# Two-block transformer kernel: values of the last attention stationary and split in two, probabilities scaled by GpSimd, a new order of its units, x kept in DRAM

## What is computed

```python
s_c = einsum("bqgid,bngd->bqgin", qc, k_cmp) * scale      # 31 compressed keys
p_c = masked_softmax(s_c, m_c)
o_c = einsum("bqgin,bngd->bqgid", p_c, v_cmp)
...
p_s = masked_softmax(s_s, m_s)        # selected branch: with 512 tokens all 8 blocks are selected
o_s = einsum("bqginl,bqgnld->bqgid", p_s, vg)
...
p_w = masked_softmax(s_w, m_w)        # window of 512: all earlier tokens
o_w = einsum("bqgik,bkgd->bqgid", p_w, vw)
return g[..., 0:1] * o_c + g[..., 1:2] * o_s + g[..., 2:3] * o_w
```

## Time and profile before

| | |
|---|---|
| median of 3 runs | 2189.94 us |
| profiled execution, its own time | 2193.54 us |
| its span | 2191.7 us |
| PE busy | 2092.1 us (95%) |
| DVE busy | 1007.5 us (46%) |
| ACT busy | 748.0 us (34%) |
| POOL busy | 0.2 us (0%) |
| queries of p = 0, first matmul to last rotation | 1768.7 to 1817.7 us |
| rounds, up to the first step of the last product | 1817.7 to 2138.5 us |
| last product and final norm | 2138.5 to 2191.7 us |

### The profile page before, as it was taken

The page is one execution under the profiler, slowest core; times in us unless marked ns, Lnnn a source line. Parts: engine busy times, 40 slices in busy tenths (PEclk is TensorE's granted clock), DMA queues, the critical chain, the costliest instruction groups (busy, mean ns, idle before and its releaser), DMA issues.

```text
span 2191.7 us, 23331 instructions
## 1 busy us (share of the span) xinstructions
PE 2092.1 (95%) x9943; PEld 1703.2 (78%) x9943; DVE 1007.5 (46%) x1342; ACT 748.0 (34%) x1143; POOL 0.2 (0%) x4
## 2 busy tenths in 40 slices
PE   7999999999999999999999999999999988988888
PEld 6899975778787887788888788888887765666666
DVE  4443444424343346542344555555545535555443
ACT  4554551332323233331242222222222123345542
POOL 0000000000000000000000000000000000000000
PEclk9999997999999999999999999999999998999999
DMA  5212122122222222333333333333333350000100
GB/s 192 78 58 77 59 76 67 61 98 77 82 96 75 89 95 87 97 96 96 96 96 96 96 96 96 96 96 96 96 96 112 99 136 20 20 20 20 39 11 39
DMA packets 177384, 177.15 MB, mean 81 GB/s; under 512 B 4609, under 2 KB 154369, under 8 KB 177281
## 3 DMA queue, kind: packets, MB, share of 16 engines
q1 hardware_dynamic: 175088, 170.31, 24.7%
q10 hardware_dynamic: 2192, 5.35, 0.9%
HBM read 171.46 MB, written 2.10 MB: 79 GB/s over the span
## 4 chain that ended last, share of the span: by engine, by line
PE 83%; DVE 7%; ACT 6%; issue 3%; DMA 1%; ACTq 0%; SPq 0%; DVEq 0%
PE bank L743 70%; PE bank L992 3%; ACT wh L1041 2%; PE bank L963 2%; DVE wl L1467 2%; PE bank L846 1%; PE bank L976 1%; ACT tmp L1025 1%; ACT pb L1025 1%; PE bank L837 1%; PE bank L827 1%; PE bank L965 0%; PE bank L887 0%; DVE sl L1926 0%; PE bank L948 0%
## 5 line engine op out<-in xcount | busy, mean ns | idle before, releaser
L743 PE MATMUL bank<-xh,wh 128*128 128x512 f32 x1352 | 553.3, 409 | 1.0 <-DVE wl L1467 1.0
L743 PE MATMUL bank<-xh,wl 128*128 128x512 f32 x1352 | 532.2, 394 | 0.0
L743 PE MATMUL bank<-xl,wh 128*128 128x512 f32 x1352 | 532.0, 394 | 0.0
L1467 DVE TENSOR_TENSOR wl<-raw,wh 128x2048 fp32r<-128x2048 f32 (+2 forms) x158 | 351.5, 2227 | 382.9 <-ACT wh L1041 382.9
L1041 ACT CAST wh<-raw 128x2048 fp32r<-128x2048 f32 (+2 forms) x158 | 292.6, 1854 | 410.5 <-PE bank L743 404.2
L743 PEld LDWEIGHTS bank<-xh,wh 128*128 128x128 f32 x1352 | 257.0, 190 | 60.9 <-issue 8.3
L743 PEld LDWEIGHTS bank<-xl,wh 128*128 128x128 f32 x1352 | 257.0, 190 | 57.8 <-issue 6.0
L743 PEld LDWEIGHTS bank<-xh,wl 128*128 128x128 f32 x1352 | 256.5, 190 | 55.9
L743 PE MATMUL bank<-wh,xh 128*128 128x512 f32 x512 | 212.9, 416 | 0.0
L743 PE MATMUL bank<-wh,xl 128*128 128x512 f32 x512 | 202.3, 395 | 0.0
L743 PE MATMUL bank<-wl,xh 128*128 128x512 f32 x512 | 202.1, 395 | 0.0
(11 more groups left out here) (243 smaller groups left out, 2406.7 us busy)
## 6 DMA issues: line engine op xcount, KB each, us to landing
raw<-in_w_in SPq DMA_DIRECT2D x50, 1024.0 KB, 4.9
raw<-in_a_w_in SPq DMA_DIRECT2D x32, 1024.0 KB, 5.4
raw<-in_w_up SPq DMA_DIRECT2D x16, 1024.0 KB, 5.4
raw<-in_w_down SPq DMA_DIRECT2D x16, 1024.0 KB, 5.8
raw<-in_w_proj_b SPq DMA_DIRECT2D x8, 1024.0 KB, 5.0
raw<-in_a_w_out SPq DMA_DIRECT2D x8, 1024.0 KB, 5.8
raw<-in_w_out SPq DMA_DIRECT2D x4, 1024.0 KB, 5.2
raw<-in_w_kv SPq DMA_DIRECT2D x4, 1024.0 KB, 4.9
```

What stands on the lines that cost most here:

```text
L743: m = e.matmul(o, p, q, start=k == 0 and n == 0, stop=k == K - 1 and n == 2)
L1467: m = e.tensor_tensor(lo, r, hi, ALU.subtract)
```

## The change

- **Values.** `values_n` now has the values stationary: `v2` holds, for each block of keys, branch and group, 128 columns, 64 with the low and 64 with the high part of the values (ACT writes the high, DVE the low, `vsw`). What moves is the transposed probabilities, split in two by ACT (`th`, a copy rounded to fp32r) and DVE (`tl`, the rest). Low half of the output and high half lie on partitions 0 to 63 and 64 to 127; both branches, both parts and the compressed branch add up in one bank for each group f. Units of one branch with the same heads form a group; for qb = 2, 3 two units make one call of `values_n` with 256 columns.
- **Normalizing.** Since all branches add up in one bank, each unit's probabilities must be scaled before they are transposed. DVE inverts the sums of each unit, and GpSimd multiplies the probabilities in place by the inverse and the gate (`rate`, 128 instructions).
- **Rounds.** A unit is (p, qb, branch, first head, count), again 44. Its parts lie in four rounds: scores, `rate`, `turn_n`, `values_n`. Six buffers hold probabilities. The banks: three for scores, two for transposes, two for sums, one for the filler tiles.
- **Gather.** ACT copies the high half of the bank to `stage`, DVE adds it to the low half and writes `oT`, already transposed. `gated` needs no transpose any more.
- **Compressed branch.** Four heads are transposed apart (8 transposes where 2 were), the result is split in two, and the values are 32-row stationary fp32r matmuls with 512 columns. Its scores are all done ahead: three before the first unit, four some rounds before p = 1.
- **Filler.** `query_steps(1)` is moved before `end kv`, and the eight `x_out` into it; ACT writes x to DRAM (`x_mid`, 8 DMAs), SP reads it back after `end nsa`. The fill in the rounds is `nz` alone, with its Silu in two groups of four. `nz` and `bo` weights use two raw slots of three; the third is used for probabilities.
- **Scale.** The scale of the scores is multiplied into the keys, and the maximum is taken negated, so that L1929 is gone.

The core of the diff:

```diff
+    main = query_steps(1)
+    o += placed(main, [(2 + 4 * n, ("x_out", *divmod(n, 2))) for n in range(8)])
     o.append(("end", "kv"))
...
+    for qb in range(3):
+        o.append(("cmp_scores", 0, qb))
+    done = 0
+    for r in range(len(UNITS) + 5):
+        if r - 3 in at.values():
+            o.append(("cmp_values", *[k for k, u in at.items() if u == r - 3][0]))
+        for G in GROUPS:
+            if GROUPS[G][-1] == r - 3:
+                o.append(("values_n", *G))
+                if G == LAST_GROUP[G[0], G[1]]:
+                    o.append(("gather", G[0], G[1]))
+        if 0 <= r - 2 < len(UNITS):
+            o.append(("turn_n", r - 2))
+        if 0 <= r - 1 < len(UNITS):
+            o.append(("rate", r - 1))
+        if r < len(UNITS):
+            o.append(("scores_n", r))
...
+        if r >= 3:
+            n = 32 * (r - 2) // 19 if r <= at[1, 0] else 32 + (len(fill) - 32) * (r - at[1, 0]) // 22
...
# tensor: values
-                    for k in range(qb + 1):
-                        w.wait_ge(*told("out_a", ("vsw", k)))
-                        m = e.matmul(bank[:, x * 64:x * 64 + 64], t[:, j * N + k * 128:j * N + (k + 1) * 128],
-                                     vsN[:, n, k, g * 64:(g + 1) * 64], start=k == 0, stop=k == qb)
+                for k in range(qb + 1):
+                    w.wait_ge(*told("out_d", ("vsw", k)))
+                    for x, t in enumerate(pair_of(G, f)):
+                        m = e.matmul(bank_of("acc", (p, qb, f))[:, i0 * 128:(i0 + cnt) * 128], v2[:, k, n * 4 + p * 2 + f, :],
+                                     t[:, 0:cnt * (qb + 1) * 128].rearrange("p (i k q) -> p k i q", i=cnt, q=128)[:, k],
+                                     start=False, stop=last and k == qb and x == 1)
...
# tensor: transposes wait for GpSimd
+                bank = take("turn_n", ("turn_n", u, f), ("lo_n", u, f))
+                w.wait_ge(*told("rated", u, f))
...
# scalar: high part of the transposed probabilities
+                e.copy(pair_of(G, f)[0][:, o:o + m], bank_of("turn_n", ("turn_n", u, f))[:, 0:m]).then_inc(
+                    *tell("hi_n", u, f))
...
# vector: low part, inverse of the sums, gather
+                e.tensor_tensor(lo[:, o:o + m], bank_of("turn_n", ("turn_n", u, f))[:, 0:m], hi[:, o:o + m],
+                                ALU.subtract).then_inc(*tell("lo_n", u, f))
...
+            w.wait_ge(*told("exp_n", u, 1))
+            e.reciprocal(wt[:, 2, :, c:c + cnt], wt[:, 1, :, c:c + cnt]).then_inc(*tell("rc", "nsa", u))
...
# gpsimd
+            w.wait_ge(*told("rc", "nsa", u))
+            w.wait_ge(*told("gts"))
+            for f in range(2):
+                c, t = f * 8 + n * 4 + i0, probs_n[(2 * u + f) % 6]
+                w.wait_ge(*told("exp_n", u, f))
+                for j in range(cnt):
+                    x = t[:, j * N:(j + 1) * N]
+                    m = e.tensor_scalar(x, x, wt[:, 32 + c + j:33 + c + j],
+                                        gts[:, qb, (p * 2 + f) * 4 + i0 + j, 1 + n:2 + n], ALU.mult, ALU.mult)
+                m.then_inc(*tell("rated", u, f))
```

More of the change, by code:

```diff
@@ L386, in make_order @@
-    rounds = [flat(parts) for parts in skewed(items)]
-    fill = query_steps(1)
-    for n in range(26):
-        o += rounds[n]
-        m = 1 + (n % 3 == 0)
-        o += flat(fill[:m])
-        fill = fill[m:]
-    o += flat(fill) + flat(rounds[26:28])
-    fill = flat([steps(("nz", f)) for f in range(8)]) + [[("gated", f)] for f in range(4)]
-    for r in rounds[28:]:
-        o += r + flat(fill[:3])
-        fill = fill[3:]
-    o += flat(fill)
+    at, extra, fill = {}, [], []
+    for r, (p, qb, n, i0, cnt) in enumerate(UNITS):
+        at.setdefault((p, qb), r)
@@ new lines, in make_order @@
+    for f in range(8):
+        tile = steps(("nz", f))
+        fill += tile[:-1] + [tile[-1] + ([("silu", x) for x in range(f - 3, f + 1)] if f % 4 == 3 else [])]
+    fill += [[("gated", f)] for f in range(4)]
+    for qb in range(3):
[15 more added lines that the diff above has]
+            o.append(("scores_n", r))
+        if r == 1:
+            o.append(("cmp_scores", 0, 3))
+        if at[1, 0] - 6 <= r < at[1, 0] - 2:
+            o.append(("cmp_scores", 1, r - at[1, 0] + 6))
+        for (p, qb), u in at.items():
+            if r == u + 1:
+                o.append(("cmp_turn", p, qb))
+        if r >= 3:
+            n = 32 * (r - 2) // 19 if r <= at[1, 0] else 32 + (len(fill) - 32) * (r - at[1, 0]) // 22
+            n = min(n, len(fill))
+            o += flat(fill[done:n])
+            done = max(done, n)
@@ L942, in cmp_values @@
         def cmp_values(p, qb):
-            bank = take("aux_n", ("cmp_values", p, qb), ("oo_cmp", p, qb))
-            w.wait_ge(*told("nT_cmp", p, qb))
-            w.wait_ge(*told("vcB"))
-            t = nT[NT_AT["cmp", p, qb] % 4]
+            w.wait_ge(*told("vc_lo"))
             for f in range(2):
-                m = e.matmul(bank[:, f * 256:f * 256 + 256], t[:, f * 128:f * 128 + 128],
-                             vcB[:, p * 2 + f, :, :].rearrange("p j d -> p (j d)"), start=True, stop=True)
+                bank = take("acc", (p, qb, f), ("gathered", p, qb, f))
+                w.wait_ge(*told("pc_lo", p, qb, f))
+                r = slice(32 * f, 32 * f + 32)
+                for x in range(2):
+                    m = e.matmul(bank[:, :], vc[r, p * 2 + f, :], pc[r, x, :], start=x == 0, stop=False)
@@ new lines, in scores_n @@
+                c = f * 8 + n * 4 + i0
+                w.wait_ge(*told("nmx_n", u, f))
+                if u >= 3:
+                    w.wait_ge(*told("turn_n", u - 3, f))
+                else:
+                    after("kv")
+                    for x in range(2):
+                        w.wait_ge(*told(f"x_mid{x}", 3, x))
+                for j in range(cnt):
+                    m = act(t[:, j * N:(j + 1) * N], bank[:, j * N:(j + 1) * N], ACT.Exp, bias=wt[:, c + j:c + j + 1],
+                            accum=wt[:, 16 + c + j:17 + c + j])
@@ L1382, in nz, with gather @@
+        def gather(p, qb):
+            for f in range(2):
+                w.wait_ge(*told("pv_n", *LAST_GROUP[p, qb], f))
+                if (p, qb) != CMP[0]:
+                    w.wait_ge(*told("gathered", *CMP[CMP.index((p, qb)) - 1], f))
+                e.copy(stage[f], bank_of("acc", (p, qb, f))[64:128, :]).then_inc(*tell("stage", p, qb, f))
         def nz(f):
@@ L2035, in all_engines @@
         vector(dve)
+        pool(gp)
         sync(sp)
-    all_engines(*[Counter() for _ in range(4)])
+    all_engines(*[Counter() for _ in range(5)])
     S_.counted = True
@@ L2054, in _ @@
         vector(e)
+    @block.gpsimd
+    def _(e):
+        pool(e)
     @block.sync
```

478 lines of the change are left out of this document (244 added, 234 removed).

## The result

The changed kernel took 2198.95 us (median of 7 runs, 2197.58 to 2200.29), the kernel before, in runs beside it, 2191.74 (2189.86 to 2195.01). The ratio is 1.0032, interval 1.0020 to 1.0044: **slower by 0.3%**, where 1.3% faster was forecast. The profiled execution took 2198.45 us, its span is 2196.6.

The account below looks back on a forecast made before the run. TensorE, busy 95% of the span, was taken as the bound. Rounds: work 238, idle 38, clock 18 make 294 against 320.8, -27; with -1 ahead -28; 2193.5 - 28 - 3.6 gives 2162 us, range 2138 to 2198.

Parts of the forecast that it names:

- rival C: GpSimd's scaling in the rounds' loop takes above 1.4 us at 512 columns; at 2.6 us, 2209 us; chance 0.12.
- (1): End of the second query block: two rotations through one bank make PE wait 4.8 us.
- (2): Start of rounds: three compressed softmaxes, exponentials, inverse and scaling while PE has only two units' scores: 10 us.
- (3): Four compressed softmaxes before p = 1: DVE's round of 6.7 us exceeds PE's; 5 us of waits.
- (4): Some 5 weight splits hold DVE 2.3 us each and ACT nearly as long, in fuller queues: 7 us.
- (5): Between blocks: both banks of sums must be gathered before the next block, 7 times 1: 6 us.
- (6): Drain of the last unit at the end of the rounds: 5 us, where 4.10 and 2.86 stood before.
- 2.8 us + X: Chain from one unit's transposes to the next's; X, GpSimd's first scaling, taken near 1.0 us, hidden up to 1.4.
- The clock loss stays near 18: Rounds: the loss to the 1.2 GHz level, 19 us before, hardly changes and adds 18 us to the sum.
- rival B: Nothing gained: 256 columns cost near 0.2 us, or the rounds' clock is near 0.85; 2188 us, chance 0.12.
- Rival A: Waits go too: the rounds' idle falls to 20 us and clock loss to 10; 2136 us, chance 0.16.
- Rival D: GpSimd stands still during DVE's two-input weight-split subtractions, five times: +5 to +11 us, 2170 us; chance 0.08.

Follow-up runs that it names:

- e4: Changed kernel without GpSimd's scaling of the two big branches' probabilities, transposes waiting for the exponentials alone: 2192.47 us, ratio 1.0003.
- e9: Changed kernel with compressed scores in the two banks of the transposes, spread over round ends, behind filler where a round has some: 2178.47 us, ratio 0.9942.
- e2: Changed kernel with filler steps of the gate tiles from round 0 on, three in each of the first three rounds: 2191.26 us, ratio 0.9995.
- e5: Changed kernel plus 180 small bf16 matmuls, result unused, where PE waited at the start of the rounds: 2195.18 us, ratio 1.0020.
- e10: e9 with filler from round 0 on, three steps in round 0 and seven by round 3: 2175.16 us, ratio 0.9923.
- e11: e10 with the weight splits of the rounds cut into four pieces: 2174.86 us, ratio 0.9919.
- e12: e11 with the last rotation of the first query block moved three steps into the second: 2168.20 us, ratio 0.9893.
- e8: Changed kernel with the four weight splits in the rounds cut into four pieces, three filler steps apart: 2192.36 us, ratio 0.9998.

## Why the prediction was wrong

**Right: the work.** 27.1 us went, or 25 to 32 over all kernels with the same PE instructions; forecast were 28 in the rounds and 1 to 2 with what lies ahead. The values of 256 columns start each 0.12 us at full clock, as taken between bounds of 0.105 and 0.23. TensorE in query block 2:

```profile
2056.50 0.28 PE L1027 MATMUL bank<-th,v 128*128 128x256 f32 x1
2056.62 0.28 PE L1027 MATMUL bank<-tl,v 128*128 128x256 f32 x1
2056.74 0.28 PE L1027 MATMUL bank<-th,v 128*128 128x256 f32 x1
```

x through DRAM cost nothing, with no wait of PE on its read. VectorE is busy 167 us and ACT 156 in the rounds (forecast 190 and 165): enough room on the mean, as said. One base figure is off by 2 us: the 19 us of clock loss before take the whole 320.8 us, and over PE's busy 285.65 it is 17.

**Right: GpSimd's price, and rival C fell.** GpSimd at 512 and 128 columns, groups by form:

```profile
L2065 POOL TENSOR_SCALAR tmp<-tmp,rs 128x512 f32<-128x512 f32 x22 | 17.7, 813 | 64.2 <-DVE rs L1995 64.2
...
L2065 POOL TENSOR_SCALAR tmp<-tmp,rs 128x128 f32<-128x128 f32 x24 | 10.4, 452 | 1882.0 <-DVE rs L1995 1882.0
...
L2065 POOL TENSOR_SCALAR raw<-raw,rs 128x512 f32<-128x512 f32 x10 | 7.6, 774 | 23.6 <-DVE rs L1995 23.6
```

0.77 to 0.81 us, below the 1.0 taken and far below the 1.4 from which it would set the round. The Trainium skill, "GPSIMD Engine Reference", "Performance versus the Vector engine", gives 769 ns as the best case for 512 elements, beside the slower figure for two inputs from which the 1.1 us in the prediction came. The rows agree with the first; here the two factors are one value per partition, and no run has two full inputs to compare. POOL's busy time is 77.6 us and not about 50. And the cost was not nothing: e4 puts it at 7 us, in short rounds and at the drain, where this link lies on the chain.

**Half right: the single waits.** (1) The second query block's rotation waited 4.83 us, forecast 4.8. (2) The start of the rounds, to 1878.51: 10.6, forecast 10. (3) The four compressed blocks before p = 1: 2.70 + 1.85 + 1.85 + 3.22 = 9.6, forecast 5. (4) Behind the first three weight splits: 2.28 + 3.47 + 2.26 = 8.0, forecast 7. (5) The banks of sums: no wait, forecast 6. (6) The drain: 11.4, forecast 5. With many small ones the rounds have 51.3 us of idle PE, forecast 38, and over the whole stretch it rose by 20.1 where I had 3. Of (3) the cause was wrong too. I counted VectorE's round of 6.7 us with a softmax in it, and not which bank each block takes. Two of the three waits of (2) after 1863 have the same cause: 2.31 us twice, each for an exponential; the third is for the compressed branch's low part, which holds a bank of the transposes. I had read the ring of three banks and never followed two consecutive turns of it.

For (6) I took the waits of before as the measure. Half of it, 5.41 us, stands behind weight split, table load and Silu group on ACT. I had counted the grouping as 15 us saved on ACT and not as 5.4 us in one piece ahead of the high parts; no run takes this piece away alone. The other half is the last unit's chain, which now has maximum, exponentials, inverse, GpSimd, transposes, high part and low part. The chain of 2.8 us + X in the prediction stood there to be laid out end to end, and I used it for the steady rounds alone.

**The step that failed** is the sentence "The clock loss stays near 18". It rose from 22.8 to 35.5 us (since the gate tile). With the 17 us of idle time beyond the forecast (terms 3 and 6 of the waits, and many small ones) these 14 us are nearly the whole miss, and either of them gone would have left a gain. Both signs that the prediction names for this came: a mean clock of 0.85 and idle time far from 38 us. I took clock loss as a property of the kernel, while it moves with the order of the work. The largest piece is the start: the level fell in the wait of 4.83 us, wait (1), which I had priced as idle time alone, and stayed down for 40 us, so that the 29.6 us of busy PE there were about 14 us of loss. The first 40 us of the rounds before (from 1817.7, behind the wait of 4.82) had a clock of 0.79 and 8 us of loss. The earlier trace rows had this in it: its two rotations take 2.08 us.

How long the level stays down behind the same wait, the rows show, and they don't show by what rule: 40 us in the changed kernel, with 10 to 11 us of idle in pieces of 0.4 to 2.3; 32 us in e9, with 0.4 us of idle in the first 14; 19 us in e2, where filler starts in round 0 but behind three compressed blocks; 12 us in e5, filled with matmuls; 9 us in e10 and e11 and 4 in e12, with filler right behind the first scores. So idle time alone doesn't set it: the first 40 us of e9 have less of it (6.0 us, clock 0.60) than those of e12 (7.4 us, 0.87). What the runs support is that matmuls one right behind another, soon after the wait, bring the clock back sooner. The profile of before had a row on this too: 0.86 in the stretch ahead of the rounds, which rival B named. The Trainium skill, "TensorE: Matmul & The Clock Gate", "A second HAM failure mode: psum-queue depth-cycling", describes a case near this one, a kernel that cycles through banks, where short idles between groups of matmuls make the clock swing between its levels. The trace agrees for 1950 to 2000 us, where the clock falls and rises between such waits and has a mean of 0.83. At the start of the rounds it does not swing but stays down. Reading it before would have made B likelier.

**Rival B** (clock near 0.85, 2188 us) is nearest: the clock of the rounds is 0.85, as it said, and the values' price, its other form, is not the cause. It missed the time by 11 us, since it kept the 38 us of waits. **Rival A** was wrong as a whole. **Rival D** did not come as described: GpSimd was idle during all four weight splits of the rounds. A small form of it is real, see below.

How far waits and clock can be told apart stays partly open. e5 gives back 7 to 8 us of clock by the accounting, against 4.4 us of work that fell into no wait; e9 shows that 15 us of waits can go with 2 us of clock; e2, e4 and e8 gave 7 to 8 us each, and two of them on top of e9 only 4 to 5. These losses overlap, so no list of them adds up to the 37 us between forecast and result.

## What to carry to other kernels

When work that is independent in data moves to another place in an engine's order, follow the ring of banks for two turns at that place: a small product behind a large one can wait for the large one's consumer. Behind a wait of several microseconds of TensorE (here 4.8), bound the cost of the busy time that follows from above at the 1.2 GHz level, look in the rows how long it stayed there, and put independent matmuls there first. When you group small work on an engine, ask what then stands behind the group in one piece. Try a repair on the whole kernel again after another has gone in, since what was worth 7 us alone may be worth nothing then.
